# Folding a modulation by whole 1024-column vectors on VectorE alone, spread by a table of weight tiles, with a rotation table built on GpSimd

## The reference

```python
cond = silu(c)
for i in range(2):
    mod = (cond @ ada_w[i] + ada_b[i])[:, None, :]
    shift1, scale1, gate1, shift2, scale2, gate2 = split(mod, 6)
    h = rmsnorm(x, norm1_g[i]) * (1 + scale1) + shift1
    y = diff_attention(h, ...) if i == 0 else axial_gqa(h, ...)      # 8 heads each
    x = x + gate1 * y
    h = rmsnorm(x, norm2_g[i]) * (1 + scale2) + shift2
    x = x + gate2 * ((silu(gate) * up) @ f_w_out[i])                 # gate, up = h @ f_w_in[i]
x = rmsnorm(x, final_g)
# then a third block: gated spatial mixing beside windowed attention, and a feed-forward with a short convolution
```

## Time and profile before

| what | us |
|---|---|
| median of 3 runs | 1160.98 (1153.46 to 1162.39) |
| the profiled execution | 1156.39 |
| its span | 1154.6 |
| TensorE busy (matmuls) | 1033.8 |
| VectorE busy | 793.4 |
| ScalarE busy | 541.4 |
| GpSimd busy | 112.7 |
| the chain that ended last: TensorE / VectorE / DMA / ScalarE | 73% / 16% / 5% / 4% |

### The profile page before, as it was taken

How to read it: one execution, slowest core, us unless ns; L and a number is a source line. 1 busy time by engine, 2 the same in 40 slices (tenths; PEclk the granted TensorE clock), 3 DMA queues, 4 the chain that set the end, 5 groups by cost and what they waited for, 6 DMA issues and landing times.

```text
span 1154.6 us, 13079 instructions
## 1 busy us (share of the span) xinstructions
PE 1033.8 (90%) x4856; PEld 850.4 (74%) x4856; DVE 793.4 (69%) x1145; ACT 541.4 (47%) x869; POOL 112.7 (10%) x116
## 2 busy tenths in 40 slices
PE   2699679999999965789999999899999989999997
PEld 2578457788878854677788878688878768888886
DVE  6778996787768879957755575655654546777653
ACT  1444462744443362545644433557454437545442
POOL 2100760000000046500000000100000000000000
PEclk9999879999999997999999999899999989999999
DMA  8797622697879655323766685376543336665551
GB/s 303 230 320 264 207 79 73 192 306 253 271 276 326 234 175 180 125 68 110 247 184 183 204 299 177 119 237 195 154 125 110 128 109 187 190 187 177 175 195 38
DMA packets 137078, 219.84 MB, mean 190 GB/s; under 512 B 9107, under 2 KB 77960, under 8 KB 137016
## 3 DMA queue, kind: packets, MB, share of 16 engines
q1 hardware_dynamic: 135728, 216.05, 57.6%
q0 software_dynamic: 960, 2.86, 0.9%
q10 hardware_dynamic: 328, 0.12, 0.0%
HBM read 217.94 MB, written 1.05 MB: 190 GB/s over the span
## 4 chain that ended last, share of the span: by engine, by line
PE 73%; DVE 16%; DMA 5%; ACT 4%; issue 2%; POOL 1%; SPq 0%; DVEq 0%; POOLq 0%; ACTq 0%
PE bank L1659 13%; PE bank L1661 13%; PE bank L1660 13%; PE bank L1674 5%; PE bank L1676 5%; PE bank L1675 5%; DVE w_lo L977 3%; DMA ada<-in_ada_w 3%; PE bank L1704 2%; PE bank L1705 2%; PE bank L1706 2%; DVE ada_acc L998 2%; ACT w_hi L575 2%; DVE wgt L1272 1%; PE bank L1759 1%
## 5 line engine op out<-in xcount | busy, mean ns | idle before, releaser
L977 DVE TENSOR_TENSOR w_lo<-raw,w_hi 128x1024 fp32r<-128x1024 f32 x312 | 382.3, 1235 | 254.5 <-ACT w_hi L575 253.2
L575 ACT ACTIVATE w_hi<-raw 128x1024 fp32r<-128x1024 f32 x312 | 327.5, 1059 | 434.2 <-PE bank L1661 256.4
L1659 PE MATMUL bank<-w_hi,h_hi 128*128 128x512 f32 x768 | 308.4, 402 | 6.3 <-DVE h_lo L1047 6.0
L1661 PE MATMUL bank<-w_hi,h_lo 128*128 128x512 f32 x768 | 301.7, 393 | 0.0
L1660 PE MATMUL bank<-w_lo,h_hi 128*128 128x512 f32 x768 | 301.6, 393 | 0.0
L1659 PEld LDWEIGHTS bank<-w_hi,h_hi 128*128 128x128 f32 x768 | 145.9, 190 | 37.4 <-issue 7.9
L1661 PEld LDWEIGHTS bank<-w_hi,h_lo 128*128 128x128 f32 x768 | 145.7, 190 | 31.4
L1660 PEld LDWEIGHTS bank<-w_lo,h_hi 128*128 128x128 f32 x768 | 146.0, 190 | 29.7 <-issue 0.8
L998 DVE SCALAR_TENSOR_TENSOR ada_acc<-ada,cond,ada_acc 128x512 f32<-128x512 f32 x140 | 105.3, 752 | 8.5 <-DMA ada<-in_ada_w 4.8
L1674 PE MATMUL bank<-w_hi,u_hi 128*128 128x512 f32 x216 | 86.1, 399 | 3.5 <-DVE act_u L1302 2.7
L1676 PE MATMUL bank<-w_hi,u_lo 128*128 128x512 f32 x216 | 84.3, 390 | 0.0
(11 more groups left out here) (265 smaller groups left out, 1316.5 us busy)
## 6 DMA issues: line engine op xcount, KB each, us to landing
ada<-in_ada_w SPq DMA_DIRECT2D x96, 512.0 KB, 5.1
raw<-in_f_w_in SPq DMA_DIRECT2D x176, 256.0 KB
raw<-in_w_in SPq DMA_DIRECT2D x46, 512.0 KB
raw<-in_f_w_out SPq DMA_DIRECT2D x44, 512.0 KB
raw<-in_w_up SPq DMA_DIRECT2D x88, 256.0 KB
raw<-in_a_w_qkv SPq DMA_DIRECT2D x24, 512.0 KB
raw<-in_w_down SPq DMA_DIRECT2D x22, 512.0 KB
raw<-in_b_w_qkv SPq DMA_DIRECT2D x12, 512.0 KB
```

The source lines that it names most:

```text
L575: nc.scalar.activation(w_hi[:, m % SPL], raw[:, m % RAW], ACT.Copy).then_inc(hi_done, 1)
L977: ve.tensor_tensor(w_lo[:, m % SPL], raw[:, m % RAW], w_hi[:, m % SPL].bitcast(F32), ALU.subtract).then_inc(lo_done, 1)
L1659: mm(o, hi, w_hi[:, s, k], start=(u == 0 and k == 0), stop=False)
L1661: last = mm(o, lo, w_hi[:, s, k], start=False, stop=(u == 3 and k == 1))
```

## The change

A modulation load is now one 128-row part with 1024 columns; eight loads make a whole vector (a shift, a scale or a gate), twelve vectors in all. One VectorE instruction folds a load, TensorE sums a vector with eight 1-column matmuls, one addition takes it. All 96 folds are VectorE's, and GpSimd's `fold` and `ada_prod` are gone. Vectors 1 and 3 accumulate in `gate_row`, the others in `ada_acc`, which now is one vector wide.

Where a load, a fold, a sum and a taking stand is one table by tile number: load a is issued ahead of weight load q, and folded right after `low(q)`. Loads 34, 35 and 80 to 83 are folded inside the two attentions. Weight loads and subtractions themselves keep their order.

GpSimd builds `table_b`: it waits for step OUT_0+14 instead of QKV_B-1, loads the inputs, and does the 20 products ahead of `root(1)`. VectorE's `table()` is gone; it waits for `table_ok` before the keys.

```diff
-LOOP_FOLD, LOOP_REDUCE, LOOP_TAKE = {0: 0, 2: 1, 3: 2, 5: 3}, {7: 0}, {7: 0}
-OUT_FOLD = {5 * (n // 4) + n % 4 - n // 12: n for n in range(16)}
+VECTORS = 12
+def fold_table():
+    after = dict(zip(range(16, 34), (6, 8, 9, 11, 12, 14, 15, 16, 18, 19, 20, 22, 23, 24, 26, 27, 28, 29)))
+    after.update({36: 30, 37: 31, 38: 32, 39: 33})
+    for a0, q0 in ((40, 39), (48, 52), (56, 65), (64, 78)):
+        after.update({a0 + n: q0 + n * 4 // 3 for n in range(8)})
+    after.update(dict(zip(range(72, 80), (92, 94, 96, 97, 104, 105, 106, 107))))
+    after.update({84 + n: 116 + n for n in range(4)})
+    after.update({88 + n: 130 + 3 * n for n in range(8)})
+    return after
+FOLD_AFTER = fold_table()
+LOAD_BEFORE = {**FOLD_AFTER, **{a: 115 for a in range(80, 84)}, 34: 30, 35: 31, 36: 32, 37: 32, 38: 33}
+REDUCE_AFTER = {12: 2, 23: 3, 46: 5, 59: 6, 72: 7, 85: 8, 104: 9, 147: 11}
+TAKE_AFTER = {19: 2, 55: 5, 68: 6, 81: 7, 94: 8, 111: 9, 156: 11}
...
             def slot_free(m, turn=None):
                 m = at(m, turn, LOOP)
+                for a, q in sorted(LOAD_BEFORE.items()):
+                    if q == m:
+                        load_ada(a)
                 if m >= RAW:
                     sp.wait_ge(lo_done, m - RAW + 1)
...
+                g, k = divmod(a, 8)
+                layer, j = divmod(g, 6)
                 if a >= ADA_SLOTS:
+                    sp.wait_ge(ada_done, a - ADA_SLOTS + 1)
+                src = ada_w[layer][k * P:(k + 1) * P, j * D:(j + 1) * D].rearrange("p (a n) -> p a n", a=2)
...
-            for a in range(28, 36):
-                fold(a)
-
             for first, end in HEADS_A:
...
-            pool.wait_ge(mm_done, QKV_B - 1)
+            pool.wait_ge(mm_done, OUT_0 + 14)
             pool.dma_start(rope_b_sb[:], rope_b.rearrange("(t p) a d -> p t a d", p=P)).then_inc(late_in[0], 16)
             pool.dma_start(gain_b[:, 0, :], qnorm_g[0].partition_broadcast(P)).then_inc(late_in[0], 16)
             pool.dma_start(gain_b[:, 1, :], knorm_g[0].partition_broadcast(P)).then_inc(late_in[0], 16)
+            pool.wait_ge(late_in[0], 48)
+            for a in range(2):
+                for t in range(T):
+                    nc.gpsimd.tensor_tensor(table_b[:, t, a, 0], rope_b_sb[:, t, 0], gain_b[:, a], ALU.mult)
+                    for lo, hi in ((0, 32), (32, 0), (64, 96), (96, 64)):
+                        last = nc.gpsimd.tensor_tensor(table_b[:, t, a, 1, lo:lo + 32], rope_b_sb[:, t, 1, lo:lo + 32],
+                                                       gain_b[:, a, hi:hi + 32], ALU.mult)
+            last.then_inc(table_ok, 1)
             root(1)
...
-            for a in range(76, 79):
-                fold(a)
...
-            for a in range(79, 82):
-                fold(a)
...
-                fold(82 + half_)
...
                 ve.tensor_tensor(w_lo[:, m % SPL], raw[:, m % RAW], w_hi[:, m % SPL].bitcast(F32),
                                  ALU.subtract).then_inc(lo_done, 1)
+                if m in TAKE_AFTER:
+                    take_vector(TAKE_AFTER[m])
+                for a, q in FOLD_AFTER.items():
+                    if q == m:
+                        fold(a)
+
+            def fold(a):
+                g, k = divmod(a, 8)
+                acc, w = acc_of(g), ada[:, a % ADA_SLOTS].rearrange("p a n -> p (a n)")
+                v_.wait_ge(ada_in[a % ADA_SLOTS], 16 * (a // ADA_SLOTS + 1))
+                if k == 0:
...
+                    ve.tensor_scalar(acc, w, cond[:, 0:1], None, ALU.mult).then_inc(ada_done, 1)
+                else:
+                    v_.wait_ge(ada_done, a)
+                    ve.scalar_tensor_tensor(out=acc, in0=w, scalar=cond[:, k:k + 1], in1=acc, op0=ALU.mult,
+                                            op1=ALU.add).then_inc(ada_done, 1)
...
+                if i in (8, 9):
+                    fold(26 + i)
...
             for m in range(12):
-                if m == 1:
-                    table()
                 if m == K_STEP_B:
+                    v_.wait_ge(table_ok, 1)
                     square_and_swap(8, 10, 1, 0)
...
+                if 5 <= i < 9:
+                    fold(75 + i)
...
+            def reduce_vector(g):
+                pe.wait_ge(ada_done, 8 * (g + 1))
                 if g:
+                    pe.wait_ge(ada_col, g)
+                for q in range(8):
+                    last = mm(sums_of(g)[:, q:q + 1], acc_of(g)[:, q * P:(q + 1) * P], ones[:, 0:1], start=True, stop=True)
                 last.then_inc(ada_red, 1)
```

More of the change, by code:

```diff
@@ L412, in _, with acc_of, sums_of @@
             sp.wait_ge(stored, 32 * T)
[L416 to L425, removed]
+        def acc_of(g):
+            return gate_row[:] if g in (1, 3) else ada_acc[:].rearrange("p a n -> p (a n)")
+        def sums_of(g):
+            return bank[0 if g < 2 else 6][:, 0:8]
         @block.gpsimd
@@ L1287, in _ @@
                 low(m + SPL)
-                k = m - WO_A
-                fold_step(7, k, steps={1: 8, 2: 9, 3: 10}, takes={1: 0, 3: 1})
-            fold(39)
             def gains_2():
-                take_group(9)
-                make_gains(N2_V, 10)
+                take_vector(4)
+                make_gains(N2_V, 4)
             boundary(0, 0, 0, IN_0, gains, mod[:, 24:32], gated=0, before=gains_2)
@@ L1751, in transposes, with reduce_after @@
                             last.then_inc(t_done, 1)
-            def reduce_group(g, turn=None):
-                pe.wait_ge(ada_done, at(8 * (g + 1), turn, 8))
+            def reduce_vector(g):
+                pe.wait_ge(ada_done, 8 * (g + 1))
                 if g:
-                    pe.wait_ge(ada_col, at(g, turn, 1))
-                for q in range(4):
-                    last = mm(bank[sum_bank(g)][:, q:q + 1], ada_acc[:, acc_slot(g), q * P:(q + 1) * P], ones[:, 0:1], start=True, stop=True)
+                    pe.wait_ge(ada_col, g)
+                for q in range(8):
+                    last = mm(sums_of(g)[:, q:q + 1], acc_of(g)[:, q * P:(q + 1) * P], ones[:, 0:1], start=True, stop=True)
                 last.then_inc(ada_red, 1)
-            def reduce_step(g, j, turn=None, steps=LOOP_REDUCE):
-                if j in steps:
-                    reduce_group(g + steps[j], turn)
+            def reduce_after(m):
+                if m in REDUCE_AFTER:
+                    reduce_vector(REDUCE_AFTER[m])
             def gate(n, h):
@@ L1918, in _ @@
                 wide(QKV_B + m, m % 4, m // 4 % 2, 3)
-                reduce_step(19, m, steps=B_REDUCE)
+                reduce_after(QKV_B + m)
                 if m in (4, 9):
@@ L1923, in _ @@
             qk_transposes_b(1, 5)
[L1925 removed]
+            pe.wait_ge(ada_col, 10)
             qk_transposes_b(2, 6)
```

168 lines of the change are left out of this document (42 added, 126 removed).

## The result

The changed kernel takes 1113.34 us (median of 4 runs, 1110.82 to 1116.48); the kernel before took 1160.62 in the same set. The ratio is 0.961, with a 95% interval of 0.958 to 0.964. Measured twice more, the changed kernel gave 1115.47 and 1114.55 us.

What follows compares the result with a forecast made beforehand. TensorE bounds the first projection and feed-forward; VectorE, slowed by GpSimd, the first attention and second projection. Gains 14.6 + 1.4 + 3.4 + 17.5 + 0 = 36.9 us off 1156.39 give 1119.5; forecast median 1121, range 1106 to 1138.

Steps and rivals of the forecast that it cites:

- The fold, 1.30 us: All loads: one 1024-column fold on VectorE takes 1.30 us, between 0.75 and 1.50.
- nothing moves: Feed-forward: 36 loads cost VectorE 47 us instead of 54, hidden by TensorE's matmuls, so no time changes.
- First attention, 18.7 - 2.6 - 1.5: First attention: heads without GpSimd's folds gain 18.7 us, folds 34 and 35 lose 2.6, TensorE's low clock 1.5; net 14.6.
- The rival of the low clock: Both attentions: TensorE's short bursts at 1.2 GHz become the bound, 1137 us; chance 0.08.
- First projection, 1.4: First block's projection: TensorE's wait for a reduction's accumulator goes, gaining 1.4 us, bounds -1 and 3.
- The transfers' rival: First projection: at 275 GB/s the 23.1 MB take 84 us, not 77, and reductions wait, 1128 us; chance 0.07.
- The boundary, 3.4: Boundary between blocks: earlier table inputs free root(1), ending TensorE's wait for the scaled rows, gaining 3.4 us.
- The table on GpSimd, 6 us: Before the boundary: GpSimd's 20 table products take 6 us, between about 4 and 25, and should finish before root(1).
- What VectorE loses meanwhile lies beside matmuls: Before the boundary: VectorE's slowdown during GpSimd's table work is hidden by TensorE's matmuls and costs nothing.
- Second projection, 24.2 - 5.2 - 1.5: Second projection: VectorE saves 24.2 us, four added folds cost 5.2, new waits 1.5; net 17.5, bounds 11 and 24.
- The wait for the keys: Second projection: TensorE still waits 4 to 6 us for the scaled keys.
- Second attention, 0: Second attention: folds 80 to 83 cost at most 5.2 us, cancelled by GpSimd's departing work; 0, bounds -5 and 3.

Runs made afterwards that it cites:

- the second of the two table runs: The changed kernel with the table's 20 products back on VectorE and their inputs loaded only after step QKV_B-1, as before: 1122.91 us.
- the feed-forward runs: The changed kernel with extra, unread GpSimd folds in the first feed-forward: eight folds 1126.26 us, two folds 1114.17 us.
- the first feed-forward run: The changed kernel with eight extra GpSimd folds, on a tile nobody reads, in the first feed-forward from step 44 on: 1126.26 us.

## Why the prediction was right, and where it was short

The range held, and the mechanism is shown: GpSimd's instructions put back bring the time back (47.8 us), at the two places that the stretches named. The sum was 6.5 us short on the profiled executions, and the misses hardly cancel: every large term fell short, and only the second attention, 0 for -1.4, went the other way. One step of it is loose: the prediction puts the median 0.4% above the profiled execution, which is 4.5 us on 1119.5 and makes 1124, but it says 1121. Step by step:

*The fold, 1.30 us.* Measured 1.278. The feed-forward, "nothing moves": 0.3.

*First attention, 18.7 - 2.6 - 1.5.* Head 1 to head 6 took 16.9 us, where the prediction had 15.9 and 0.3 for a diagonal: 18.0 gained for 18.7. That leaves 0.7 at most for the 1.5 of the clock. Folds 34 and 35 cost 1.1 for 2.6 (from head 7's reduction to the transposes 11.25 us before, 12.33 after). So the deductions were too large, and the heads' own gain was right. The rival of the low clock fell: less idleness brought the clock back (0.76 to 0.89) instead of laying it bare.

*First projection, 1.4.* No wait for `ada_acc` is left, and 2.6 us came. The transfers' rival fell: 347 GB/s at a share of 0.96 is what the estimate of 343 from the earlier trace rows said can be had, not the mean of 275.

*The boundary, 3.4.* The wait is confirmed by the second of the two table runs. The stretch gave more: TensorE's second run of steps behind the boundary starts at 417.41 before and 392.17 after, 5.2 us gained since the first `res`. From the first of these matmuls to the second run it is 6.34 us before, at a clock of 0.51 from 411 to 414, and 5.34 after, at 1.00: the clock behind the wait is 1.0 of the 1.8 missing.

*The table on GpSimd, 6 us.* Its 20 products took 10.1 (0.56 us for the wide, 0.52 for the narrow in the mean). Undisturbed ones are 0.45 for a wide one and 0.88 for four narrow ones, 5.3 us in all, so 6 was right for an engine left alone; but VectorE holds GpSimd too, and four narrow ones took 4.28 beside its subtractions and folds. The term was mis-sized, but the table ended at 376.8 for the 381.5 at which `root(1)` came. "What VectorE loses meanwhile lies beside matmuls" was right for ten microseconds and wrong as a rule, as the feed-forward runs show.

*Second projection, 24.2 - 5.2 - 1.5.* It gave 19.5 for 17.5; with the boundary 24.7 for 20.9. The durations came as forecast (0.42 and 0.69). Two things were off. The wait for the keys, forecast at 4 to 6 us, is gone; in its place stand 3.4 us for the diagonal behind the fifth step, since folds 76 to 79 stand around it in VectorE's order. And the sum had no term for the clock: before, this stretch ran at 0.83, now at 1.00. I take the missing 2.0 us for that and for the new waits of 1.5, but no run parts the two. The fold term was right in kind: taking the folds out again brought 3.7 to 5.3 for the 5.2 counted.

*Second attention, 0.* It lost 1.4, within the bounds of -5 to 3; the four folds there are 0.74 and three times 1.28 us, and what GpSimd's release gave back stands against them.

The expectation that failed outright, that of the first feed-forward run, was about a thing that the prediction had left loose, how much GpSimd a stretch bound by TensorE can bear. The answer had been in the rows: VectorE's idle time plus the lead in split tiles, against the growth of each instruction that reads two operands from SBUF.

## What to carry to other kernels

Before giving elementwise work to GpSimd, list what VectorE runs beside it: each instruction with two SBUF operands can be held for a whole GpSimd instruction, and so can a `tensor_scalar` from SBUF to SBUF (0.75 to 1.78 us); those that read PSUM are not. Such work is free only where VectorE has idle time and the engine behind it a lead; short pieces into stretches bound by matmuls, none into an attention or a projection where VectorE ends last. A wait of TensorE costs more than itself when the clock falls behind it (3.4 + 2.7 us at the boundary). And a long mean of a well-known shape (1.48 for 1.22, 2.08 for 0.69 us) is the sign to look for on the page of a kernel that does it already.

## What the chip showed that I had not expected

- The hold is per instruction: VectorE's three operations ended 0.29 us after GpSimd's three. It isn't a shared rate, so many short VectorE operations beside few long GpSimd ones lose the most (256-column products 0.42 to 1.27, or up to 2.1 us).
- GpSimd is held too: its 512-column addition took 1.33 us beside short VectorE work, 2.14 beside 1024-column subtractions.
- GpSimd's small products are short when VectorE leaves it alone (0.45 us for 128x128, four of 128x32 in 0.88), and several times longer when it doesn't: four of 128x32 in 4.28.
- Memsets of GpSimd leave two-operand instructions of VectorE alone and slow a one-operand `tensor_scalar` of four columns from 0.17 to 0.62 us in the mean. A short instruction right behind a held one reads long too; it is not held itself.
- One core alone drew 347 GB/s over 35 us at a DMA share of 0.96.
